# Low part one place later at the norms, and the layer norms' last sums moved from GpSimd to TensorE

## The chip, the cores and the metric

The kernel runs on one core of a Trainium2 chip. The time is device microseconds of one execution, from the first to the last instruction and what lies around them. The engines are TensorE (PE; PEld is its weight load), VectorE (DVE), ScalarE (ACT), GpSimd (POOL) and SyncE (SP, which issues the DMAs of the weight stream).

## What is computed

Two transformer stacks, one behind the other, on 512 tokens of width 1024, in float32. The first has two layers (a mixer of gated linear attention and sparse attention, a gated spatial mixer, and a squared-ReLU MLP after each), with a root-mean-square norm before and after every part. The second has one layer with layer norms: neighbourhood and windowed attention behind a joint input projection, an output projection, and an MLP. What matters for the change are the norms:

```python
def _rms_norm(x, g):
    y = xf * lax.rsqrt(jnp.mean(xf * xf, axis=-1, keepdims=True) + NORM_EPS)
    return (y * g).astype(x.dtype)

h = h + _rms_norm(m, norm_g[layer, 1])                       # first stack
f = _squared_relu_mlp(_rms_norm(h, norm_g[layer, 2]), ...)
h = h + _rms_norm(f, norm_g[layer, 3])

def layer_norm(x, g, b):                                     # second stack
    mu = jnp.mean(xf, axis=-1, keepdims=True)
    xc = xf - mu
    var = jnp.mean(xc * xc, axis=-1, keepdims=True)
    y = xc * lax.rsqrt(var + LN_EPS) * g + b
h = layer_norm(x, ln0_g, ln0_b)
h = layer_norm(ALPHA * h + attn_out, ln1_g, ln1_b)
h = layer_norm(ALPHA * h + ffn_out, ln2_g, ln2_b)
```

## The kernel before

Activations lie transposed: 128 partitions by 8 blocks of the width (KC = 8) by 512 tokens. Weights come as a stream of 321 panels of 128 by 1024 through a ring of four places. Every float32 operand is split in a high and a low part: for a panel ScalarE copies the high part (`act_split`, L321) and VectorE subtracts it for the low part (`dve_split`, L328); a product is then three matmuls (high by high, high by low, low by high). "Split q" below is that of the panel q of the next stage. TensorE signals a panel's end with `panel_done`, VectorE a split with `lo_done`.

The order on every engine is written out by hand, and semaphores join the engines. The stages are mix0 (three of them), ffn0, sgu_in, sgu_out, ffn1, mix2_in, mix2_gate, mix2_branch, mix2_out and ffn2. Between two stages stands a norm, and to keep TensorE at work the tokens are taken in two halves of 256 (`half(s)`): the last four panels of a stage run as a tail (`pe_tail`), first for half 0 and then for half 1, while the norm of half 0 goes on; the first four panels of the next stage run as a quad (`pe_quad`), first half 0 block by block and then half 1. `pe_quad` puts a number of constant products of the identity into an unused bank ahead of each half (`pe_hold`, L442, counts in `HOLD`, L444), before it waits for the first block.

Root-mean-square boundary (`dve_boundary`, `act_boundary`; r = 0, 1, 2 stand before ffn0, sgu_in and ffn1). Once the root of a half is there, VectorE takes the reciprocal (`dve_post_rs`, L545), and for each of eight blocks the scale (`dve_post_scale`, L548), the add into h (`dve_post_add`, L553) and the low part of the block before (`lo`, L562). ScalarE makes the high part in between (`hi`, L589). `STEPS` (L411) is VectorE's order, with the four splits and the tail's sums among them; "last" is the low part of block 7.

Layer norm m = 0 (before mix2_in, on h), 1 (before ffn2, on h), 2 (the end, on acc). The mean: GpSimd adds blocks into `part` (`pool_mean_full`, L668, for the first four blocks at full width where m > 0; `pool_mean_half`, L678, one block of a half), and TensorE multiplies `part` and the last block by a matrix of 1/1024 (`pe_mean`, L683 and L685). VectorE subtracts (`dve_centre`, L691), ScalarE squares (`act_var_square`, L698), GpSimd adds the squares of blocks 0, 2, 4, 6 (`pool_var`, L707), and TensorE sums the odd ones and that sum (`pe_var`, L713 and L715). Then the root on ScalarE (`act_var_sd`, L720), the reciprocal (`dve_var_rs`, L725) and the scale (`dve_norm`, L728) on VectorE, the high part and the bias on ScalarE (`act_ln_out`, L733, L736), and the low part on GpSimd (`pool_ln_lo`, L740).

The ends that matter: at m = 0 the norm behind ffn1 (r = 3: `act_post_square`, `pool_post_half`, `pe_post`, `act_post_sd`, `dve_post_rs`, and VectorE's `post3`, L2380) runs into the layer norm, and halves of both are interleaved by hand in all engines' lists (GpSimd L1211 to L1240, TensorE from L1611, ScalarE from L1937, VectorE from L2391). At m = 1 and 2, `pe_ln` hands the mean and the squares to the tail and the quad as things to do after a given part, and `dve_ln` is VectorE's order.

GpSimd's queue also issues DMAs: behind the adds of boundary r = 1 those of wst and bs, and behind `pool_var` of m = 0 those of the rope table and the first biases of the neighbourhood attention.

## Time and profile before

| | us |
|---|---|
| median of 3 runs | 2292.1 |
| lowest and highest | 2281.51, 2295.62 |
| the profiled execution | 2285.85 |
| its span, first to last instruction | 2283.9 |
| TensorE busy in the span | 2201.7 (96%) |
| VectorE busy | 1103.5 (48%) |
| ScalarE busy | 852.5 (37%) |
| GpSimd busy | 237.3 (10%) |
| mean granted TensorE clock, as a share of full speed | 0.983 |

The profile is of one execution. A time in it counts from the span's start. A matmul's end is modelled, so neighbouring matmuls overlap in it; the distance of two starts is the better measure. A constant or float32 product is recorded as two matmuls. In the timeline the bracket at a line's end holds the idle time of the engine before it and what ended it. Idle time of an engine off the path costs nothing.

### The profile page before, as it was taken

How to read it: one execution, taken by the hardware profiler on the slowest of the kernel's cores; microseconds unless marked ns; L12 is line 12 of the kernel's file. 1: busy time of each engine (PE TensorE's matmuls, PEld its weight loads, DVE VectorE, ACT ScalarE, POOL GpSimd, SP SyncE). 2: the span in 40 equal slices, each digit the busy share in tenths (PEclk: the TensorE clock that was granted, in tenths of full speed). 3: DMA queues.
4: the chain of work that ended last, by engine and by line, in shares of the span. 5: the costliest groups of instructions: out<-in, count | busy, mean ns of one | idle time of the engine just before them, and what ended most of it. 6: DMA issues, size and time to landing. Idle time of an engine off the chain costs nothing.

```text
span 2283.9 us, 28971 instructions
## 1 busy us (share of the span) xinstructions
PE 2201.7 (96%) x11040; PEld 1801.1 (79%) x11040; DVE 1103.5 (48%) x1798; ACT 852.5 (37%) x1411; POOL 237.3 (10%) x220
## 2 busy tenths in 40 slices
PE   7998989999999999999999999999999999999997
PEld 5877768888888788889888888876677788888886
DVE  5546555633433736626443445545544445443344
ACT  6324433432323433324332232533476326232232
POOL 2001002010001100310100003401100123000002
PEclk9999988999999999999999999999999999999999
DMA  4223000333222232222332322221111222322331
GB/s 165 90 68 93 19 10 28 102 93 102 92 92 92 93 102 82 86 92 74 102 101 92 94 90 81 84 73 51 34 49 47 83 84 65 111 93 92 100 93 37
DMA packets 52400, 184.51 MB, mean 81 GB/s; under 512 B 5904, under 2 KB 8096, under 8 KB 52288
## 3 DMA queue, kind: packets, MB, share of 16 engines
q1 hardware_dynamic: 49968, 173.39, 24.0%
q0 software_dynamic: 2320, 9.55, 1.3%
q8 instruction: 79, 1.29, 0.2%
q14 instruction: 33, 0.27, 0.0%
HBM read 180.82 MB, written 2.10 MB: 80 GB/s over the span
## 4 chain that ended last, share of the span: by engine, by line
PE 86%; DVE 8%; ACT 3%; POOL 1%; issue 1%; DMA 0%; SPq 0%; ACTq 0%; DVEq 0%; POOLq 0%
PE ps L354 55%; PE ps L941 4%; PE ps L908 3%; PE ps L929 3%; PE ps L1586 3%; PE ps L431 3%; PE ps L1508 3%; PE ps L463 2%; PE ps L919 2%; DVE ring L328 2%; DVE h L553 1%; DVE xa L562 1%; PE ps L1381 1%; ACT ring L321 1%; PE ps L1481 1%
## 5 line engine op out<-in xcount | busy, mean ns | idle before, releaser
L354 PE MATMUL ps<-xa,ring 128*128 128x512 f32 x3192 | 738.9, 391 | 0.0
L354 PEld LDWEIGHTS ps<-xa,ring 128*128 128x128 f32 x3192 | 598.2, 188 | 127.2 <-issue 3.0
L321 ACT ACTIVATE ring<-raw 128x1024 fp32r<-128x1024 f32 x321 | 337.7, 1054 | 513.3 <-PE ps L354 415.8
L328 DVE TENSOR_TENSOR ring<-raw,ring 128x1024 fp32r<-128x1024 f32 x321 | 409.5, 1277 | 245.7 <-ACT ring L321 245.2
L354 PE MATMUL ps<-xb,ring 128*128 128x512 f32 x2208 | 517.2, 395 | 0.0
L354 PEld LDWEIGHTS ps<-xb,ring 128*128 128x128 f32 x2208 | 414.4, 188 | 100.5
L835 DVE TENSOR_TENSOR ffsq<-relu 128x512 f32<-128x512 f32 x96 | 66.3, 691 | 180.3 <-ACT relu L794 180.2
L852 DVE TENSOR_TENSOR acc<-acc,ps 128x512 f32<-128x512 f32 x68 | 46.8, 688 | 207.7 <-PE ps L354 207.7
L941 PE MATMUL ps<-xa,ring 128*128 128x512 f32 x432 | 118.6, 413 | 0.0
L463 PE MATMUL ps<-xa,ring 128*128 128x256 f32 x768 | 97.1, 285 | 11.6 <-POOL xa L740 5.4
L941 PEld LDWEIGHTS ps<-xa,ring 128*128 128x128 f32 x432 | 77.9, 192 | 37.9 <-issue 23.5
L463 PEld LDWEIGHTS ps<-xa,ring 128*128 128x128 f32 x768 | 93.4, 191 | 15.9 <-POOL xa L740 7.4
L794 ACT ACTIVATE relu<-ps 128x512 f32<-128x512 f32 x64 | 38.1, 595 | 180.8 <-PE ps L354 180.8
L838 DVE TENSOR_TENSOR xb<-ffsq,xb 128x512 fp32r<-128x512 f32 x96 | 66.5, 692 | 76.0 <-ACT xb L786 76.0
L1508 PE MATMUL ps<-ring,xa 128*128 128x512 f32 x384 | 90.8, 397 | 2.6 <-DVE xa L562 2.5
L1508 PEld LDWEIGHTS ps<-ring,xa 128*128 128x128 f32 x384 | 72.4, 191 | 20.0 <-DVE xa L562 4.4
L431 PE MATMUL ps<-xb,ring 128*128 128x256 f32 x576 | 70.2, 283 | 0.0
L431 PEld LDWEIGHTS ps<-xb,ring 128*128 128x128 f32 x576 | 69.3, 188 | 0.5
L1017 DVE RECIPROCAL stat<-stat 128x1 f32<-128x1 f32 x128 | 20.9, 163 | 100.1 <-PE ps L929 98.4
L516 POOL TENSOR_TENSOR part<-part,xf 128x512 f32<-128x512 f32 x8 | 14.3, 1793 | 496.7 <-ACT xf L500 496.7
L786 ACT ACTIVATE xb<-ffsq 128x512 fp32r<-128x512 f32 x96 | 59.9, 624 | 11.9 <-DVE ffsq L835 11.7
L969 ACT ACTIVATE n_p<-ps,stat 128x128 f32<-128x128 f32 (+3 forms) x64 | 33.7, 527 | 77.1 <-DVE stat L1005 76.8
(334 smaller groups left out, 2442.5 us busy)
## 6 DMA issues: line engine op xcount, KB each, us to landing
raw<-in_stream SPq DMA_DIRECT2D x321, 512.0 KB, 3.5
c_w<-in_cmp_w POOLq DMA_DIRECT2D x8, 512.0 KB, 4.2
t<-in_rpb POOLq DMA_DIRECT2D x8, 448.0 KB, 3.6
h<-in_x SPq DMA_DIRECT2D x8, 256.0 KB, 8.4
out_y<-h SPq DMA_DIRECT2D x16, 128.0 KB, 1.9
cons<-in_con SPq DMA_DIRECT2D x1, 738.0 KB, 4.3
wst<-in_w_s POOLq DMA_DIRECT2D x1, 512.0 KB, 4.6
bs<-in_b_s POOLq DMA_DIRECT2D x1, 512.0 KB, 5.3
```

The costliest lines, as they stand in the source:

```text
L321: nc.scalar.activation(ring[:, m % RING, 0], raw[:, m % RING], ACT.Copy).then_inc(hi_done, 1)
L328: nc.vector.tensor_tensor(ring[:, m % RING, 1], raw[:, m % RING], ring[:, m % RING, 0].bitcast(F32), ALU.subtract).then_inc(lo_done, 1)
L354: mm = nc.tensor.matmul(bank[:, :], ring[:, n % RING, w, k * P:(k + 1) * P], operand[:, k, xx], start=(i == 0 and w == 0 and xx == 0), sto ...
L431: mm = nc.tensor.matmul(ps[bank][:, half(q % 2)], ring[:, n % RING, w, k * P:(k + 1) * P], operand[:, k, xx, half(s)], start=(k == 0 and w ...
L463: mm = nc.tensor.matmul(ps[QUAD[c]][:, half(s)], ring[:, (n0 + k // 2) % RING, w, at_w:at_w + P], xa[:, k, xx, half(s)], start=(k == 0 and ...
L835: nc.vector.tensor_tensor(ffsq[:, j % 2], relu[:, j % 2], relu[:, j % 2], ALU.mult)\
L838: nc.vector.tensor_tensor(xb[:, j, 1], ffsq[:, j % 2], xb[:, j, 0].bitcast(F32), ALU.subtract).then_inc(sem("ff_lo"), 1)
L908: mm = nc.tensor.matmul(bank[:, 0:nk], q, k, start=True, stop=not masks)
L929: mm = nc.tensor.matmul(ps[2][:, 0:HD], turned[:, u_ % 2, j * P:(j + 1) * P], v[j], start=(j == 0), stop=(j == nk // P - 1))
L941: mm = nc.tensor.matmul(ps[BANK[n]][:, :], ring[:, n % RING, w, k * P:(k + 1) * P], operand[:, k, xx], start=(k == 0 and w == 0 and xx == ...
L1508: mm = nc.tensor.matmul(ps[V_BANKS[g][t]][:, :], xa[:, k, xx, t * P:(t + 1) * P], ring[:, n % RING, w, (k % 2) * T:(k % 2) * T + T], start ...
L1586: mm = nc.tensor.matmul(ps[BANK[n]][:, :].rearrange("p (t d) -> p t d", t=TB), ring[:, n % RING, w, k * P:(k + 1) * P], y_block(KC * i + k ...
```

## The change

- In `dve_boundary` the add of a block comes right behind its scale, and the low part of the block before comes after both. The order in `STEPS` stays.
- The mean of a layer norm: `pool_mean_half` goes. At m = 0 TensorE multiplies all eight blocks of a half by the mean matrix, each as it is ready; at m = 1 and 2 it takes GpSimd's `part` (blocks 0 to 3) and then blocks 4 to 7.
- The squares: `pool_var` goes; TensorE sums all eight.
- `HOLD`: ffn0 and ffn1 (0, 4) to (0, 3), mix2_in (10, 9) to (7, 9), ffn2 (5, 9) to (3, 3).
- At m = 0, half 0 of the layer norm comes ahead of half 1 of the norm behind ffn1: on TensorE its squares before `pe_post(3, 1)`, on ScalarE its root before that one's, on VectorE centring before split 0, and reciprocal and scales before the post norm's reciprocal and first two blocks.
- At m = 1 and 2, the squares of half 1 are summed after block 5 of the next quad's half 0 instead of after block 7 (at the end there is no quad; they stand behind the mean as before).

```diff
@@ -160,7 +160,7 @@
 MIX_AT = {4: (0,), 5: (1,), 6: (2, 3), 7: (4,), 8: (5, 6), 9: (7,), 10: (8, 9), 11: (10,), 12: (11,), 13: (12,), 14: (13,),
           15: (14, 15)}
 PRE_AT = {"ffn0": KC, "sgu_in": 3 * KC, "ffn1": 5 * KC}
-MEAN_PART = (0, 12, 21)
+MEAN_PART = (0, 0, 3)
 
 
 def blocks_beside(i, count, units):
@@ -441,7 +441,7 @@
             for _ in range(count):
                 nc.tensor.matmul(bank[:, :], ident, cons[:, CON["scan"]:CON["scan"] + HT], start=True, stop=True)
 
-        HOLD = {"ffn0": (0, 4), "ffn1": (0, 4), "mix2_in": (10, 9), "ffn2": (5, 9)}
+        HOLD = {"ffn0": (0, 3), "ffn1": (0, 3), "mix2_in": (7, 9), "ffn2": (3, 3)}
 
         def pe_quad(pe, name, ready, after):
 
@@ -572,9 +572,9 @@
                         dve_post_rs(dve, chain, r, s)
                     elif what == "step":
                         dve_post_scale(dve, r, s, i, g_post)
+                        dve_post_add(dve, r, s, i)
                         if i >= 1:
                             lo(s, i - 1)
-                        dve_post_add(dve, r, s, i)
                     elif what == "last":
                         lo(s, KC - 1)
                     elif what == "out":
@@ -668,22 +668,15 @@
                 nc.gpsimd.tensor_tensor(part[:, :], src[:, 0] if k == 1 else part[:, :], src[:, k], ALU.add)\
                     .then_inc(sem("mean_part"), 1)
 
-        def pool_mean_half(pool, m, s, k, src, ready):
-
-            pool.wait_ge(*ready)
-            first = m == 0 and k == 1
-            if not first:
-                done = (6 * s + k - 1) if m == 0 else (3 + 3 * s + k - 4)
-                pool.wait_ge(sem("mean_part"), MEAN_PART[m] + done)
-            nc.gpsimd.tensor_tensor(part[:, half(s)], src[:, 0, half(s)] if first else part[:, half(s)],
-                                    src[:, k, half(s)], ALU.add).then_inc(sem("mean_part"), 1)
-
         def pe_mean(pe, m, s, src, ready):
-            pe.wait_ge(sem("mean_part"), MEAN_PART[m] + (6 * s + 6 if m == 0 else 3 * s + 6))
-            nc.tensor.matmul(ps[2 - 2 * s][:, half(s)], mean_w, part[:, half(s)], start=True, stop=False)
-            pe.wait_ge(*ready)
-            nc.tensor.matmul(ps[2 - 2 * s][:, half(s)], mean_w, src[:, KC - 1, half(s)], start=False, stop=True)\
-                .then_inc(sem("mean_summed"), 1)
+            if m > 0:
+                pe.wait_ge(sem("mean_part"), MEAN_PART[m] + 3)
+                nc.tensor.matmul(ps[2 - 2 * s][:, half(s)], mean_w, part[:, half(s)], start=True, stop=False)
+            for k in range(0 if m == 0 else 4, KC):
+                pe.wait_ge(*ready(k))
+                mm = nc.tensor.matmul(ps[2 - 2 * s][:, half(s)], mean_w, src[:, k, half(s)], start=(m == 0 and k == 0),
+                                      stop=k == KC - 1)
+            mm.then_inc(sem("mean_summed"), 1)
 
         def dve_centre(dve, m, s, k, src):
             if k == 0:
@@ -697,23 +690,11 @@
                 act.wait_ge(sem("var_summed"), 2 * m + 1)
             nc.scalar.activation(squares[:, k], h[:, k, half(s)], ACT.Square).then_inc(sem("var_sq"), 1)
 
-        def pool_var(pool, m, s, squares):
-
-            for k in range(2, KC, 2):
-                pool.wait_ge(sem("var_sq"), 16 * m + 8 * s + k + 1)
-                done = 6 * m + 3 * s + k // 2 - 1
-                if k > 2:
-                    pool.wait_ge(sem("var_part"), done)
-                nc.gpsimd.tensor_tensor(part[:, half(s)], squares[:, 0] if k == 2 else part[:, half(s)], squares[:, k],
-                                        ALU.add).then_inc(sem("var_part"), 1)
-
         def pe_var(pe, m, s, squares):
-            for k in range(1, KC, 2):
+            for k in range(KC):
                 pe.wait_ge(sem("var_sq"), 16 * m + 8 * s + k + 1)
-                nc.tensor.matmul(ps[6 + s][:, half(s)], mean_w, squares[:, k], start=k == 1, stop=False)
-            pe.wait_ge(sem("var_part"), 6 * m + 3 * s + 3)
-            nc.tensor.matmul(ps[6 + s][:, half(s)], mean_w, part[:, half(s)], start=False, stop=True)\
-                .then_inc(sem("var_summed"), 1)
+                mm = nc.tensor.matmul(ps[6 + s][:, half(s)], mean_w, squares[:, k], start=k == 0, stop=k == KC - 1)
+            mm.then_inc(sem("var_summed"), 1)
 
         def act_var_sd(act, m, s):
             act.wait_ge(sem("var_summed"), 2 * m + s + 1)
@@ -1211,17 +1192,8 @@
             for q in range(3):
                 pool_post_half(pool, 3, 0, q)
 
-            def mean0(s, k):
-                pool_mean_half(pool, 0, s, k, h, (sem("h_ready"), 48 + 8 * s + k + 1))
-
-            for k in range(1, 5):
-                mean0(0, k)
-            pool_post_half(pool, 3, 1, 0)
-            pool_post_half(pool, 3, 1, 1)
-            mean0(0, 5)
-            mean0(0, 6)
-            pool_post_half(pool, 3, 1, 2)
-            pool_var(pool, 0, 0, lnsq)
+            for q in range(3):
+                pool_post_half(pool, 3, 1, q)
             pool.wait_ge(panel_done, BASE["ffn1"] + 64)
             pool.dma_start(ropes[:, :, :], rope).then_inc(sem("rope_in"), 16)
 
@@ -1232,9 +1204,6 @@
             load_rpb(1)
             for k in range(KC):
                 pool_ln_lo(pool, 0, 0, k)
-            for k in range(1, 7):
-                mean0(1, k)
-            pool_var(pool, 0, 1, lnsq)
             for k in range(KC):
                 pool_ln_lo(pool, 0, 1, k)
             for hd in range(8):
@@ -1255,19 +1224,10 @@
             def pool_ln(m, name, src, lo):
                 n0 = tail_base(name)[0]
                 pool_mean_full(pool, m, src, lambda k: (taken["dve"], READS["dve"][n0 - 4 + k + 1]))
-                for k in range(4, 7):
-                    pool_mean_half(pool, m, 0, k, src, (sem("tail_out"), tail_base(name)[1] + (k - 4) // 2 + 1))
-                for k in range(4, 6):
-                    pool_mean_half(pool, m, 1, k, src, (taken["dve"], READS["dve"][n0 + 2]))
-                pool_var(pool, m, 0, xfh)
-                pool_mean_half(pool, m, 1, 6, src, (taken["dve"], READS["dve"][n0 + 4]))
                 if lo:
-                    for k in range(KC):
-                        pool_ln_lo(pool, m, 0, k)
-                pool_var(pool, m, 1, xfh)
-                if lo:
-                    for k in range(KC):
-                        pool_ln_lo(pool, m, 1, k)
+                    for s in range(2):
+                        for k in range(KC):
+                            pool_ln_lo(pool, m, s, k)
 
             pool_ln(1, "mix2_out", h, True)
             pool_ln(2, "ffn2", acc, False)
@@ -1608,13 +1568,13 @@
                         mm.then_inc(sem("tail_a"), 1)
             pe_ffn(pe, "ffn1", pre_ready("ffn1"), sums(2)[1], 2, sums(3)[0])
 
-            pe_mean(pe, 0, 0, h, (sem("h_ready"), 48 + KC))
+            pe_mean(pe, 0, 0, h, lambda k: (sem("h_ready"), 48 + k + 1))
+            pe_var(pe, 0, 0, lnsq)
             pe_post(pe, 3, 1)
-            pe_var(pe, 0, 0, lnsq)
 
             def quad0(s, k):
                 if s == 0 and k == 7:
-                    pe_mean(pe, 0, 1, h, (sem("h_ready"), 48 + 2 * KC))
+                    pe_mean(pe, 0, 1, h, lambda i: (sem("h_ready"), 48 + KC + i + 1))
                     pe_var(pe, 0, 1, lnsq)
 
             pe_quad(pe, "mix2_in", ln_ready(0), quad0)
@@ -1674,14 +1634,14 @@
 
                 def tail(s, q):
                     if s == 1 and q == 0:
-                        pe_mean(pe, m, 0, src, (sem("tail_out"), t0 + 2))
+                        pe_mean(pe, m, 0, src, lambda k: (sem("tail_out"), t0 + k // 2 - 1))
                     if s == 1 and q == 2:
                         pe_var(pe, m, 0, xfh)
 
                 def quad(s, k):
                     if s == 0 and k == 1:
-                        pe_mean(pe, m, 1, src, (taken["dve"], READS["dve"][n0 + 4]))
-                    if s == 0 and k == 7:
+                        pe_mean(pe, m, 1, src, lambda i: (taken["dve"], READS["dve"][n0 + 2 * (i // 2) - 2]))
+                    if s == 0 and k == 5:
                         pe_var(pe, m, 1, xfh)
 
                 return tail, quad
@@ -1689,7 +1649,7 @@
             tail, quad = pe_ln(1, "mix2_out", h)
             pe_tail(pe, "mix2_out", xs, tail)
             pe_ffn(pe, "ffn2", ln_ready(1), quad, None, pe_ln(2, "ffn2", acc)[0])
-            pe_mean(pe, 2, 1, acc, (taken["dve"], READS["dve"][BASE["ffn2"] + 64]))
+            pe_mean(pe, 2, 1, acc, lambda k: (taken["dve"], READS["dve"][BASE["ffn2"] + 60 + 2 * (k // 2) - 2]))
             pe_var(pe, 2, 1, xfh)
 
         @block.scalar
@@ -1936,8 +1896,8 @@
             split_to("mix2_in", 0)
             for k in range(KC):
                 act_var_square(act, 0, 0, k, lnsq)
+            act_var_sd(act, 0, 0)
             act_post_sd(act, 3, 1)
-            act_var_sd(act, 0, 0)
             for k in range(KC):
                 act_ln_out(act, 0, 0, k, "ln0_b")
                 if k in (0, 2, 5):
@@ -2391,15 +2351,15 @@
                 post3(0, k)
                 if k in (3, 7):
                     dve_tail(dve, "ffn1", 1, k // 4, acc)
-            split_to("mix2_in", 0)
             for k in range(KC):
                 dve_centre(dve, 0, 0, k, h)
+            split_to("mix2_in", 0)
+            dve_var_rs(dve, chain, 0, 0)
+            for k in range(KC):
+                dve_norm(dve, 0, 0, k, "ln0_g")
             dve_post_rs(dve, chain, 3, 1)
             post3(1, 0)
             post3(1, 1)
-            dve_var_rs(dve, chain, 0, 0)
-            for k in range(KC):
-                dve_norm(dve, 0, 0, k, "ln0_g")
             for k in range(2, KC):
                 post3(1, k)
                 if k in (2, 4, 6):
```

## Rows read from the trace of the kernel before

**Rows 1.** The page: the chain of work that ended last, by engine.
```profile
PE 86%; DVE 8%; ACT 3%; POOL 1%; issue 1%; DMA 0%; SPq 0%; ACTq 0%; DVEq 0%; POOLq 0%
```

**Rows 2.** Timeline at ffn0's norm, second half of the tokens: start us, us, engine.
```profile
405.02 0.48 DVE L548 SCALAR_TENSOR_TENSOR acc<-acc,vecs,ps 128x256 f32<-128x256 f32 x1
...
405.54 0.42 DVE L553 TENSOR_TENSOR h<-h,acc 128x256 f32<-128x256 f32 x1
...
405.88 0.47 DVE L548 SCALAR_TENSOR_TENSOR acc<-acc,vecs,ps 128x256 f32<-128x256 f32 x1
...
406.54 0.48 DVE L562 SCALAR_TENSOR_TENSOR xa<-h,vecs,xa 128x256 fp32r<-128x256 f32 x1 [0.18 <-ACT xa L589]
...
407.93 0.49 DVE L562 SCALAR_TENSOR_TENSOR xa<-h,vecs,xa 128x256 fp32r<-128x256 f32 x1 [0.18 <-ACT xa L589]
...
415.87 1.22 DVE L328 TENSOR_TENSOR ring<-raw,ring 128x1024 fp32r<-128x1024 f32 x1 [1.52 <-ACT ring L321]
...
417.41 0.48 DVE L562 SCALAR_TENSOR_TENSOR xa<-h,vecs,xa 128x256 fp32r<-128x256 f32 x1
...
417.94 3.13 PE L463 MATMUL ps<-xa,ring 128*128 128x256 f32 x24 [1.96 <-DVE xa L562]
```

**Rows 3.** Timeline at sgu_in's norm.
```profile
780.95 10.08 PE L1508 MATMUL ps<-ring,xa 128*128 128x512 f32 x36 [2.22 <-DVE xa L562]
...
791.93 1.12 PE L1539 MATMUL ps<-part,cons 128*128 128x512 f32 x2 [0.91 <-DVE part L2281]
```

**Rows 4.** Windows: busy us and counts of PE, PEld, DVE, ACT, POOL, granted clock, DMA.
```profile
405.00:421.00 16.00, 13.85 (x107) 13.09 (x106) 12.26 (x27) 7.26 (x12) 0.00 (x0) 1.00 0.12 34
...
783.00:784.00 1.00, 1.00 (x4) 0.81 (x3) 1.00 (x2) 1.00 (x2) 0.00 (x0) 0.50 0.63 152
...
1415.00:1421.00 6.00, 6.00 (x15) 4.66 (x16) 4.41 (x10) 3.65 (x10) 2.62 (x4) 0.53 0.31 87
```

**Rows 5.** Timeline: constant products ahead of mix2_in (two records each).
```profile
1421.74 4.48 PE L442 MATMUL ps<-cons 128*128 128x256 f32 x20
```

**Rows 6.** Timeline at ffn1's end and mix2_in.
```profile
1414.94 1.22 PE L683 MATMUL ps<-part,cons 128*128 128x256 f32 x2 [3.47 <-POOL part L678]
...
1417.06 2.74 DVE L691 TENSOR_TENSOR h<-h,ps 128x256 f32<-128x256 f32 x8 [0.15 <-PE ps L685]
...
1421.94 0.45 ACT L720 ACTIVATE ps<-ps,cons 128x256 f32<-128x256 f32 x1 [1.43 <-PE ps L715]
...
1427.69 1.68 PE L463 MATMUL ps<-xa,ring 128*128 128x256 f32 x12 [1.47 <-POOL xa L740]
...
1429.13 1.22 DVE L328 TENSOR_TENSOR ring<-raw,ring 128x1024 fp32r<-128x1024 f32 x1
...
1432.03 1.76 DVE L328 TENSOR_TENSOR ring<-raw,ring 128x1024 fp32r<-128x1024 f32 x1
...
1443.40 0.70 PE L683 MATMUL ps<-part,cons 128*128 128x256 f32 x2 [2.07 <-POOL part L678]
...
1450.49 0.45 ACT L720 ACTIVATE ps<-ps,cons 128x256 f32<-128x256 f32 x1 [2.74 <-PE ps L715]
...
1455.20 11.77 PE L463 MATMUL ps<-xa,ring 128*128 128x256 f32 x96 [0.33 <-POOL xa L740]
```

**Rows 7.** Timeline at mix2_out's end and ffn2.
```profile
1892.89 0.45 ACT L720 ACTIVATE ps<-ps,cons 128x256 f32<-128x256 f32 x1 [3.27 <-PE ps L715]
...
1914.05 0.45 ACT L720 ACTIVATE ps<-ps,cons 128x256 f32<-128x256 f32 x1 [5.40 <-PE ps L715]
...
1918.76 11.77 PE L463 MATMUL ps<-xa,ring 128*128 128x256 f32 x96 [0.86 <-POOL xa L740]
```

**Rows 8.** Timeline at the end of ffn2, the last norm.
```profile
2267.19 0.68 DVE L493 TENSOR_TENSOR acc<-acc,ps 128x512 f32<-128x512 f32 x1
...
2269.90 2.73 DVE L691 TENSOR_TENSOR h<-acc,ps 128x256 f32<-128x256 f32 x8 [0.46 <-PE ps L685]
...
2275.00 0.45 ACT L720 ACTIVATE ps<-ps,cons 128x256 f32<-128x256 f32 x1 [1.92 <-PE ps L715]
```

## The prediction

> **What bounds the kernel now.** I read the chain of work that ended last first: 86% of it is TensorE, 8% VectorE [rows 1]. So a norm costs only what TensorE waits in it, and the change touches six norms: at ffn0, sgu_in and ffn1 (root mean square), at mix2_in, ffn2 and the end (layer norms). Then the timelines at the norms, and the windows for the granted clock.
>
> At ffn0, in the second half of the tokens, VectorE runs scale, low part, add for each block. A block takes 1.39 us (406.54 to 407.93), of which part is a wait for ScalarE's high part [rows 2]. TensorE keeps up until block 6, stands idle 1.96 us, and starts at 417.94 when that block's low part is done [rows 2]. At sgu_in the same gap is 2.22 us, and a second one stands at 791.93, behind sums on VectorE [rows 3]. ffn1 repeats ffn0 with the same 1.96 us.
>
> At mix2_in TensorE is idle 3.47 us before the first mean product (so its tail ended at 1411.47) and 2.07 us before the second half's [rows 6]. Here the clock matters: behind the first gap the window from 1415 to 1421 has a granted clock of 0.53, and the one from 783 at sgu_in 0.50, the lower level of 1.2 GHz; round ffn0's gap of 1.96 us it stays 1.00 [rows 4].
>
> **Prices.** A constant product is two records; 20 records take 4.48 us, the last one's own 0.38 included, so one product takes 0.43 us at the full clock [rows 5]. A block of twelve matmuls takes 1.48 us (96 in 11.77 [rows 6]).
>
> **Edit 1, low part one place later.** Now the add stands right behind its scale, which it needs: 0.52 us from start to start (405.02 to 405.54), then 0.34 to the next (405.88) [rows 2]. The low part is as long as the scale, 0.48, and overlaps alike: 0.40. The wait for ScalarE goes, since a high part of a whole period earlier is asked for. The new period is 0.52 + 0.34 + 0.40 = 1.26. Add 1 ends at 405.88 + 0.52 + 0.42 = 406.82 and add 6 five periods later at 413.1, where it ended at 414.36 (405.96 and six periods): 1.26 us earlier. The split behind it (415.87) moves with it, since ScalarE's copy follows high part 6 at once. Of step 7, low part 6 stood 0.40 behind the scale and now stands 0.52 + 0.34 = 0.86 behind: 0.46 later. Net **−0.8 us** at ffn0 and again at ffn1. The next stop is low part 7, some 0.6 us behind low part 6 and hidden by TensorE's block 6 (1.48). In the first half each of seven steps pays 0.13 us for the add behind its scale, less the waits for ScalarE that go (about 0.8): nothing on VectorE; TensorE's last two blocks there start up to 0.6 us later, which the one constant product fewer (0.43) gives back ahead of the second half. Without that cover it is +0.2. If waits and stalls cancel in the second half too, the gain is nothing; if low part 6 were not delayed it is −1.3.
>
> At sgu_in the wait that ends last is another: high part 7, two splits, copies and squares on ScalarE and sums on VectorE lead to 791.93 [rows 3]. They start with add 7, which gains 1.26 and another 0.27 (0.79 to 0.52 behind its scale). TensorE's own work ahead of 791.93 comes in 0.9 + 0.8 us earlier, so it can use it: **−1.5 us** (between −0.8 and −1.7). The loads of wst and bs on GpSimd's queue wait for the same adds and move with them; nothing else is queued there.
>
> **Edit 2, TensorE sums.** 42 sums leave GpSimd (18 at mix2_in, 12 at each other layer norm) and 42 products come to TensorE: per half 8 + 8 for 2 + 5 at mix2_in, 5 + 8 for 2 + 5 elsewhere. 13 constant products go: 41 of these four stages become 28.
>
> mix2_in, first half: the eight mean products can start at 1411.47, since all but the last block of h is added by then: 8 × 0.43 = 3.45, centring at 1414.95 for 1417.06. TensorE now waits for h block by block, with the squares, the other half's sum and mix2_in queued behind it; VectorE adds the last block some 0.3 us after 1411.47, seven products early, so nothing waits. The gap of 3.47 us goes, and with it the low clock. First square 0.9 behind, eight products, 0.2 of drain: the root at 1419.5 for 1421.94 [rows 6]. From root to TensorE's first block it is 4.71 us where nothing stands between (1914.05 to 1918.76 [rows 7]), here 5.75 since the other half's reciprocal and two steps stood there; they now stand behind. So block 0 starts at 1424.2 for 1427.69, 3.5 us earlier. But this doesn't last. Block 2 needs the split of the next panel, and VectorE reaches it only behind its reciprocal and the eight norm products (1419.5 + 0.5 + 1.8 + 8 × 0.39 = 1424.9), the other half's reciprocal (1.8), three scales and two adds (1.9): at 1428.6, done between 1429.8 and 1430.4. That is where it was before (1429.13 + 1.22 = 1430.35 [rows 6]). From there VectorE's pace, some 3.3 us for each of two further splits (1430.35 to 1433.8), rules as before, and TensorE ends two blocks behind the last split: 1430.1 + 2 × 3.35 + 3.0 = 1439.8, for 1441.33 (1443.40 less 2.07 [rows 6]). GpSimd's mean is not waited for: centring at 1439.8 + 3.6 = 1443.4, root 4.55 later at 1448.0 for 1450.49, block 0 at 1452.7 for 1455.20. **−2.5 us**. The new gap ahead of block 2, some 2.6 us, is longer than that of sgu_in, so I expect the low level behind it; it slows blocks that wait for the splits anyway, so it costs 0.1 to 1: **−2.4**. If nothing held, the gain would be 3.8 us; if the splits slip by a microsecond and the clock falls in both halves, it is nothing.
>
> Here the Trainium skill speaks against the change. A split takes 1.22 us with GpSimd at rest [rows 2] and once beside its low parts, but 1.76 there at 1432.03 [rows 6]. The GPSIMD Engine Reference (section 1, Specifications) says that GpSimd shares its SBUF interfaces with VectorE and contends with VectorE instructions that have two SBUF inputs. By that rule all splits moved beside low parts take 1.76 and the term is −1.9; by the 1.22 alone it is −2.9. The trace agrees with the rule in one of the two splits.
>
> The rope and bias loads on GpSimd's queue come some 7 us earlier, once its sums ahead of them are gone. They meet no panel load that is waited for: four panels have landed. Price nothing.
>
> ffn2: TensorE's tail carries three products more at the mean (+1.3), so centring starts 1.3 later; eight products behind one another end 0.2 sooner than four, a wait for GpSimd and a fifth, and the root goes from 1892.89 to 1894.0 [rows 7]. GpSimd has no sum left in front of its first low part, so block 0 starts 4.71 later, at 1898.7, where the profile has 1898.96. Two blocks (2.96) and five mean products (2.15) lead to 1903.8. The squares are now summed behind block 5, not 7: 1903.8 + 4 × 1.48 = 1909.7, then 3.45 + 0.2, root at 1913.35 for 1914.05: **−0.7 us** (+0.6 if the squares, due at 1909.75, come late; −1 at best). The holds ahead of it fall from 9 to 3, and TensorE waits some 0.7 us in place of 0.86 [rows 7].
>
> The end: the mean +1.3 and the squares +0.6 (three products less a wait for GpSimd and its sum) shift the first half's root by 1.9; the tail's sum on VectorE moves from 2267.19 to 2269.1 [rows 8]. Three mean products run ahead of it and GpSimd's sum is gone, but VectorE's tail sum (0.6) and other four norm products (1.6) now stand ahead of the centring: 2271.3 for 2269.90. From centring to root it was 5.1 us, at the low clock, and is 4.55 at the full one: 2275.85 for 2275.00. **+0.9 us** (0 to +2.6, the latter if the clock falls: eight products at half speed for some 3.4 us, as long as it lasted at sgu_in, cost 1.7).
>
> **Sum.** −0.8 − 1.5 − 0.8 − 2.4 − 0.7 + 0.9 = −5.3 us. Against the profiled execution's own 2285.85 us: 2280.5. The runs shown have a median of 2292.1 and a lowest of 2281.51; with the profiled one the middle of four is 2289.0. A new set of runs may fall anywhere there, so I put the level at 2289 and forecast 2284.
>
> **Rivals.**
> 1. *Slower: TensorE becomes the bound at the layer norms.* 42 products more and 13 fewer are 29 × 0.43 = 12.5 us. For it: each stands in TensorE's order, blocks behind it wait. Against it: in every layer norm TensorE has gaps of 0.9 to 3.5 us [rows 6, 7]. It decides where the products exceed the gap they fill, as in the tails of ffn2. All on the path: 2289 + 12.5 = 2301. Chance 0.08.
> 2. *The reordering does nothing*: the add's stall eats the wait that goes. Then −5.3 + 3.1 = −2.2: 2287. For it: 0.13 us stall against a 0.18 us wait. Against: the period is a sum of starts seen. Chance 0.17.
> 3. *The clock falls in the waits*, which have fewer constant products: five stretches at 1.7 us each, −5.3 + 8.5 = +3.2: 2292. For it: the gaps of 2.2 and 3.5 us. Against: ffn0's 1.96, and most new gaps are about 1 us. Chance 0.15.
> 4. *The full gain at mix2_in* (3.8, splits not in the way): 2282. Against: the walk above. Chance 0.05.
>
> The forecast has 0.55; its own range is 2276 to 2291, mostly the spread of the runs shown (14 us). The range goes from there up to rival 3: 2275 to 2295; rival 1 is left out. About 1% (23 us) is what a measurement can tell from no change. Only rival 1 with high runs or a low set could pass it: faster 0.02, same 0.95, slower 0.03.
>
> **What would show it.** Right: at ffn0 low parts 1.26 us apart and a gap near 1.2 us where 1.96 was; at mix2_in centring at once behind eight products, a wait for VectorE's split ahead of block 2, clock 1.00 in the second half's squares; at the end the last root about 0.9 later relative to the last panel. Wrong: low parts still 1.4 apart; block 2 following block 1 without a wait; a granted clock near 0.5 behind gaps of 1 us; a total off by over 8 us, which no walk here would explain.

## The result, and the profile after

| | before | after |
|---|---|---|
| median of 13 runs | 2286.91 us (2280.94 to 2296.55) | 2276.5 us (2271.09 to 2280.44) |
| profiled execution | 2285.85 us | 2271.93 us |
| its span; mean granted clock | 2283.9 us; 0.983 | 2270.2 us; 0.992 |

The ratio after to before is 0.9946, 95% interval [0.9928, 0.9964]. That is inside the 1% that was called no change, and 2276.5 us is inside the forecast's range, but the gain is 10.4 us by the medians where 5.3 were worked out. The changed kernel was measured twice more, each time with new runs of before beside it: 0.9962 [0.9949, 0.9975] and 0.9967 [0.9956, 0.9978], that is 8.7 and 7.5 us of 2283. The median of before was 2286.91 us here and 2282.51 to 2283.78 us in the four later sets of 29 to 33 runs, so some 3 to 4 of the 10.4 us look like this set's own and not the change's.

The two profiled spans differ by 13.7 us. This table cuts both at the same matmuls of TensorE's order; each entry is a difference of two starts in the trace, and behind it the time in that stretch at the lower of the clock's two levels.

| TensorE from ... to ... | before, us (low) | after, us (low) | difference |
|---|---|---|---|
| start to the output product ahead of ffn0 (code untouched) | 360.85 (29.0) | 356.51 (18.8) | -4.3 |
| ffn0's norm, to its first quad's end | 59.93 (8.5) | 59.43 (8.5) | -0.5 |
| sgu_in's norm | 63.34 (3.4) | 61.59 (0) | -1.75 |
| ffn1's norm | 52.55 (0) | 51.30 (0) | -1.25 |
| mix2_in's norm and quad | 79.02 (13.7) | 77.59 (3.4) | -1.45 |
| neighbourhood attention (untouched) | 137.62 (6.8) | 134.42 (0) | -3.2 |
| windowed attention, gates, to mix2_out (untouched) | 219.02 (6.8) | 217.45 (3.4) | -1.6 |
| ffn2's norm and quad | 61.95 (0) | 61.19 (0) | -0.75 |
| ffn2's last panels and the end | 44.34 (9.9) | 45.41 (3.9) | +1.1 |

All other stretches agree within 0.03 us. The touched ones give -4.6 us where the forecast had -5.3, each with the sign it was given. The rest, -9.1 us in this pair, stands in three stages whose code is the same.

**The profile after.** The granted clock and the chain that ended last, by engine: TensorE's share is 88%, where it was 86 [rows 1].

```profile
core 0: 2270.2 us, clock 0.992
PE 88%; DVE 8%; ACT 3%; issue 1%; POOL 0%; DMA 0%; SPq 0%; ACTq 0%; DVEq 0%
```

ffn0's norm after, second half of the tokens (timeline: start us, us, engine, line, operation; L548 is the scale, L553 the add, L562 the low part, L463 the quad's blocks):

```profile
403.63 0.42 DVE L553 TENSOR_TENSOR h<-h,acc 128x256 f32<-128x256 f32 x1
403.97 0.48 DVE L562 SCALAR_TENSOR_TENSOR xa<-h,vecs,xa 128x256 fp32r<-128x256 f32 x1
404.37 0.47 DVE L548 SCALAR_TENSOR_TENSOR acc<-acc,vecs,ps 128x256 f32<-128x256 f32 x1
404.88 0.42 DVE L553 TENSOR_TENSOR h<-h,acc 128x256 f32<-128x256 f32 x1
405.22 0.48 DVE L562 SCALAR_TENSOR_TENSOR xa<-h,vecs,xa 128x256 fp32r<-128x256 f32 x1
...
412.56 0.48 DVE L562 SCALAR_TENSOR_TENSOR xa<-h,vecs,xa 128x256 fp32r<-128x256 f32 x1
413.09 3.13 PE L463 MATMUL ps<-xa,ring 128*128 128x256 f32 x24 [0.95 <-DVE xa L562]
```

The period is 1.25 us (403.97 to 405.22), where the forecast had 1.26 and before had 1.39 [rows 2]. No wait for ScalarE is left in it. TensorE's gap is 0.95 us for 1.96.

mix2_in after. L677 are the mean products, L684 the centring, L696 the squares' products, L701 the root, L442 constant products, L328 VectorE's part of a weight split:

```profile
1403.46 3.62 PE L677 MATMUL ps<-h,cons 128*128 128x256 f32 x16
1407.12 2.74 DVE L684 TENSOR_TENSOR h<-h,ps 128x256 f32<-128x256 f32 x8 [2.24 <-PE ps L677]
1411.80 0.45 ACT L701 ACTIVATE ps<-ps,cons 128x256 f32<-128x256 f32 x1 [1.50 <-PE ps L696]
1416.51 1.69 PE L463 MATMUL ps<-xa,ring 128*128 128x256 f32 x12 [0.86 <-POOL xa L721]
1421.37 1.21 DVE L328 TENSOR_TENSOR ring<-raw,ring 128x1024 fp32r<-128x1024 f32 x1
1422.64 10.38 PE L463 MATMUL ps<-xa,ring 128*128 128x256 f32 x72 [2.54 <-DVE ring L328]
1424.26 1.75 DVE L328 TENSOR_TENSOR ring<-raw,ring 128x1024 fp32r<-128x1024 f32 x1
1427.54 1.21 DVE L328 TENSOR_TENSOR ring<-raw,ring 128x1024 fp32r<-128x1024 f32 x1
1432.86 3.62 PE L677 MATMUL ps<-h,cons 128*128 128x256 f32 x16
1436.52 2.74 DVE L684 TENSOR_TENSOR h<-h,ps 128x256 f32<-128x256 f32 x8 [6.70 <-PE ps L677]
1441.20 0.45 ACT L701 ACTIVATE ps<-ps,cons 128x256 f32<-128x256 f32 x1 [1.50 <-PE ps L696]
1445.91 7.34 PE L463 MATMUL ps<-xa,ring 128*128 128x256 f32 x59 [0.86 <-POOL xa L721]
```

The whole kernel reaches mix2_in 7.85 us sooner after, so 7.85 is to be added to compare with [rows 6]. The gap of 3.47 us is gone. In its place TensorE waits 2.54 us for VectorE's split ahead of block 2, as forecast, and behind that wait the clock is low; windows (busy us of PE, PEld, DVE, ACT, POOL, then granted clock, DMA share, GB/s):

```profile
1422.50:1427.00 4.50, 4.36 (x24) 4.36 (x25) 4.50 (x9) 2.50 (x5) 3.75 (x4) 0.62 0.38 117
1441.00:1446.00 5.00, 4.14 (x20) 3.33 (x18) 4.29 (x8) 2.39 (x6) 0.73 (x1) 1.00 0.01 3
```

The end after (L493 adds the tail's last sums; L684 and L701 as above):

```profile
2244.26 0.69 DVE L493 TENSOR_TENSOR acc<-acc,ps 128x512 f32<-128x512 f32 x1 [0.84 <-PE ps L431]
2250.49 0.45 ACT L701 ACTIVATE ps<-ps,cons 128x256 f32<-128x256 f32 x1 [4.43 <-PE ps L696]
2254.35 0.68 DVE L493 TENSOR_TENSOR acc<-acc,ps 128x512 f32<-128x512 f32 x1
2256.51 2.73 DVE L684 TENSOR_TENSOR h<-acc,ps 128x256 f32<-128x256 f32 x8
2261.28 0.45 ACT L701 ACTIVATE ps<-ps,cons 128x256 f32<-128x256 f32 x1 [1.58 <-PE ps L696]
```

From the tail's sum to the last root it is 6.93 us (2254.35 to 2261.28), where it was 7.81 (2267.19 to 2275.00 [rows 8]); the first half's root comes 0.6 later behind its own sum, and the mean products 1.3 later: +1.3 + 0.6 - 0.9 = +1.0. That is against this profile of before. The last stretch took 353.55 us there and in one other profile of before's order, counted from ffn2's first panel behind its quad, and 354.4 to 354.5 us in the seven others, with 12 to 15 us low for 9.9; after has 354.62 us. Against those seven the end lost 0.1 to 0.3 us.

### The profile page after: what moved, and what is told of

Same layout as the page of the kernel before. It is cut to its first block, busy times and chain, and to the rows that moved or that the text cites. A ratio compares the mean times of both kernels' runs of the same rounds, so it can differ in the third digit from the quotient of the medians.

```text
span 2270.2 us, 29011 instructions
## 1 busy us (share of the span) xinstructions
PE 2196.7 (97%) x11098; PEld 1800.7 (79%) x11098; DVE 1102.7 (49%) x1798; ACT 853.3 (38%) x1411; POOL 202.8 (9%) x178
## 4 chain that ended last, share of the span: by engine, by line
PE 88%; DVE 8%; ACT 3%; issue 1%; POOL 0%; DMA 0%; SPq 0%; ACTq 0%; DVEq 0%
PE ps L354 56%; PE ps L922 4%; PE ps L889 3%; PE ps L431 3%; PE ps L910 3%; PE ps L1546 3%; PE ps L1468 3%; PE ps L463 2%; PE ps L900 2%; DVE ring L328 1%; PE ps L696 1%; DVE acc L548 1%; DVE h L553 1%; PE ps L1341 1%; ACT ring L321 1%
## 5 line engine op out<-in xcount | busy, mean ns | idle before, releaser
L328 DVE TENSOR_TENSOR ring<-raw,ring 128x1024 fp32r<-128x1024 f32 x321 | 408.0, 1273 | 242.5 <-ACT ring L321 242.1
L463 PE MATMUL ps<-xa,ring 128*128 128x256 f32 x768 | 98.9, 288 | 10.9 <-DVE ring L328 3.5
L463 PEld LDWEIGHTS ps<-xa,ring 128*128 128x128 f32 x768 | 95.0, 194 | 15.3 <-POOL xa L721 4.9
L767 ACT ACTIVATE xb<-ffsq 128x512 fp32r<-128x512 f32 x96 | 59.8, 623 | 10.7 <-DVE ffsq L816 10.4
L1546 PE MATMUL ps<-yhi,ring 128*128 128x512 f32 x192 | 60.5, 395 | 0.0
```

The source lines that it names most:

```text
L328: nc.vector.tensor_tensor(ring[:, m % RING, 1], raw[:, m % RING], ring[:, m % RING, 0].bitcast(F32), ALU.subtract).then_inc(lo_done, 1)
L463: mm = nc.tensor.matmul(ps[QUAD[c]][:, half(s)], ring[:, (n0 + k // 2) % RING, w, at_w:at_w + P], xa[:, k, xx, half(s)], start=(k == 0 and ...
L1546: mm = nc.tensor.matmul(ps[BANK[n]][:, :].rearrange("p (t d) -> p t d", t=TB), ring[:, n % RING, w, k * P:(k + 1) * P], y_block(KC * i + k ...
```

## The experiments

**Theory 1**, after the result: the edits do what the walk said, and the rest is the clock in attention stages. Rivals: the edits are worth more than reckoned; the two sets of runs differ by luck; the holds matter. The first four ran side by side (before there: median 2283.56 us of 33 runs).

**The kernel before, unchanged**, as a measure of what two equal kernels differ by.

> The kernel before, unchanged, for more executions and a second profile. Theory A (the gain beyond the 4.6 us found in the changed norms is clock time in the attention stages that has nothing to do with the change): single executions lie anywhere from 2281 to 2297 us, and between two of them the time differs by about half of the difference in time at the low clock; ratio 1.000 +-0.002. Theory B (the low clock in the attention stages of before is fixed by the kernel): the second profile shows the low level at the same places as the first, 2285 to 2290 us in the median.

2282.07 us, ratio 0.9992 [0.9977, 1.0007]. Its stages repeat those of before within 0.05 us, attention with its low stretches too (137.57 and 219.02 us), but for the first: 356.84 us (18.8 low) where before had 360.85 (29.0). So the first row of the table above, -4.3 us, comes and goes between executions of one kernel and is no gain of the change. The attention rows repeat in these two profiles of before; of after's three profiles, further down, one does not repeat the others. The low stretches stood at the same places, as theory B of this run had it, but its median of 2285 to 2290 was not reached.

**The low part one place later, alone.**

```diff
                         dve_post_scale(dve, r, s, i, g_post)
+                        dve_post_add(dve, r, s, i)
                         if i >= 1:
                             lo(s, i - 1)
-                        dve_post_add(dve, r, s, i)
```

> Only the low part one place later in the three boundaries; everything else as before. Theory A, by the places read from the two profiles: ffn0 -0.5, sgu_in -1.8, ffn1 -1.2, together -3.5 us, ratio 0.9985. Theory B (the gaps made shorter also keep the clock up in most executions): -6 us or more, ratio 0.997 or less, and a mean granted clock above that of before.

2279.57 us, ratio 0.9979 [0.9969, 0.9989], between the two theories. (The profile is of its slowest execution, 2285.19 us.) ffn1's norm took 51.30 us, the change's whole 1.25. At sgu_in the sums reach TensorE 24.12 us behind the reciprocal (764.37 to 788.49), in before 25.70 (766.23 to 791.93): 1.6 sooner. But that norm's stretch gained only 0.3 (63.02 us), for now the low clock stood behind the wait instead of before it:

```profile
778.24 8.46 PE L1508 MATMUL ps<-ring,xa 128*128 128x512 f32 x36 [1.37 <-DVE xa L562]
788.49 1.12 PE L1539 MATMUL ps<-part,cons 128*128 128x512 f32 x2 [1.79 <-DVE part L2281]
790.48 9.80 PE L1508 MATMUL ps<-ring,xa 128*128 128x512 f32 x36
```

36 matmuls took 8.46 us ahead of the wait and 9.80 behind it; in before 10.08 ahead of it [rows 3]. And the neighbourhood attention took 139.91 us, 2.3 more than in before. So what an edit saves ahead may be lost behind.

**All but that: the layer norms, alone** (the low part's place and the holds of ffn0 and ffn1 as before).

> All of the change but the low part's place (and the constant products of ffn0 and ffn1, which stay at 4). Theory A: mix2_in -1.4, ffn2 -0.7, end +1.1, together -1.0 us, ratio 0.9995. Theory B (the low clock behind mix2_in's long gaps was the larger part, in more places than one profile shows): -5 us or more, ratio 0.998 or less.

2278.71 us, ratio 0.9976 [0.9965, 0.9986]. mix2_in 77.58 us (-1.45), ffn2 61.18, the end +1.0, as in after. At sgu_in, where and ahead of which this kernel is still as before, the stretch took 65.45 us, 2.1 more than before, with 4.5 us low; attention 135.09. By the medians both halves of the change gain, about 5 us each, and together 8 to 10. But the three layer norms give only some 1.1 of the 5.5 us: the ratio is the one of theory B, and in the profile (2282.3 us, among the slower executions) the other gain is 4.1 us in the two attention stages, whose code is before's.

sgu_in shows the same in a smaller way. From its norm to sgu_out's last panels, with before's code there and ahead of it, five profiles took 292.2 us with 3.4 us low, and four, this one among them, 295.4 to 295.5 us with 6.8 us low.

**The changed kernel with the old holds** (10, 9 at mix2_in, 5, 9 at ffn2, 4 for 3 at ffn0 and ffn1).

```diff
-        HOLD = {"ffn0": (0, 3), "ffn1": (0, 3), "mix2_in": (7, 9), "ffn2": (3, 3)}
+        HOLD = {"ffn0": (0, 4), "ffn1": (0, 4), "mix2_in": (10, 9), "ffn2": (5, 9)}
```

> The changed kernel with the constant products of before (4, 4, 10 and 9, 5 and 9). Theory A (the constant products end before the operand comes): as the changed kernel where they fit, later where they don't: ffn2's nine products of 3.9 us stand in a wait of some 2 us, so +2 us there and +0.5 at mix2_in, ratio to before 0.9955 to 0.996. Theory B (fewer constant products let the clock fall): faster than the changed kernel, ratio below 0.9945.

2277.73 us, ratio 0.9972 [0.9962, 0.9982]. ffn2 took 62.97 us for 61.19: nine constant products are longer than the wait they fill now. No other stage is longer by its counts. sgu_in, whose own code is that of after, took 1.6 us more with 3.4 us low behind its wait, and the ratio is above the 0.9955 to 0.996 that was expected.

**The changed kernel again**, with three others (before there: 2282.97 us of 29 runs).

> The changed kernel as it is, for a comparison beside the parts on one chip and a second profile. Theory A (each half of the change keeps its own gain, and the constant products taken out add the rest): the low part alone gave 0.9979 and the sums alone 0.9976, so 0.9945 to 0.9955. Theory B (the first comparison was a lucky one): 0.997 to 0.998, the 4.6 us of the changed norms alone. The profile: the six norms' stages as in the first profile to 0.1 us, except sgu_in; the neighbourhood attention anywhere from 134.4 to 140 us, by where the low clock falls.

2274.53 us, ratio 0.9962 [0.9949, 0.9975]; attention 134.33 and 217.42 us, every touched stage within 0.2 of the first profile.

**The changed kernel with before's order at mix2_in** (the other half's post norm ahead of the layer norm's squares, root, reciprocal and scales, split 0 ahead of the centring).

> The changed kernel with the order of before at mix2_in: on TensorE the other half's sum ahead of the squares, on VectorE its reciprocal and first two blocks ahead of the layer norm's reciprocal. Theory A (the split of the next panel is what ends the wait, so the move changes nothing behind block 1): mix2_in's stage within 0.5 us of the changed kernel's 77.6, ratio as the changed kernel. Theory B (the move carries mix2_in's gain): 1.4 us or more longer there, as long as before (79.0).

2280.86 us, ratio 0.9992 [0.9983, 1.0001]: 6.3 us more than its neighbour. At mix2_in itself it lost 1.05 us (78.62), between the 0.5 and the 1.4 of the two theories. The neighbourhood attention, in which nothing was changed, took 143.59 us, 9.3 more.

**Where that time is.** In all these kernels TensorE has one gap of 2.29 us in the neighbourhood attention, some 55 us into it (the others there are 0.8 us or less, but for one of 1.2 us at its end): the transposes of a score unit wait for its probabilities. After has it too:

```profile
1557.09 0.66 PE L900 MATMUL ps<-cons,a_p 128*128 128x128 f32 x4 [2.29 <-ACT a_p L950]
```

The windows of the 7 us behind it, in before, after, and after with the old order, one line each:

```profile
1566.38:1573.38 7.00, 7.00 (x26) 4.92 (x26) 2.60 (x6) 3.12 (x7) 0.00 (x0) 0.58 0.00 0
```
```profile
1557.09:1564.09 7.00, 7.00 (x36) 4.90 (x37) 4.10 (x10) 3.02 (x7) 0.00 (x0) 1.00 0.00 0
```
```profile
1559.04:1566.04 7.00, 7.00 (x28) 4.97 (x28) 2.59 (x6) 3.14 (x7) 0.00 (x0) 0.61 0.00 0
```

The same gap, the same work behind it, and a granted clock of 0.58, 1.00 and 0.61 (the level of 1.2 GHz for most of the window in two of them): 36 matmuls done in one, 26 and 28 in the others. **Theory 2**: whether the clock falls behind a given gap hangs on when the kernel arrives there, and a microsecond or two of work ahead of it decide. Rival: the change itself makes the attention faster by some other way (buffers, weight splits that come sooner).

**mix2_in's gaps filled in the kernel before**: eight and five constant products ahead of its two mean products.

```diff
+            pe_free(pe, BASE["mix2_in"] + 1)
+            pe_hold(pe, ps[3][:, half(0)], 8)
             pe_mean(pe, 0, 0, h, (sem("h_ready"), 48 + KC))
...
+                    pe_hold(pe, ps[3][:, half(1)], 5)
                     pe_mean(pe, 0, 1, h, (sem("h_ready"), 48 + 2 * KC))
```

> The kernel before with eight constant products in mix2_in's gap of 3.47 us and five in that of 2.07 us, so that the clock stays up; sums on GpSimd as before. Theory A (of mix2_in's gain the kept clock is the larger part): clock 1.00 from 1414 to 1452, the stage 1.5 us shorter than before's 79.0, ratio 0.999 or less. Theory B (the gain is that TensorE doesn't wait for GpSimd): within 0.4 us of 79.0.

2282.38 us, ratio 0.9997 [0.9988, 1.0006]. mix2_in took 77.75 us with no low clock at all, 1.3 less than before and only 0.15 more than the change, with GpSimd's sums still there; attention 134.41 and 217.44 as in after, with before's code. So the attention's time is reached without any of the change's edits. In this profile 3.2 us were given back at sgu_in (65.51, 4.6 low, 1.1 more behind it) and 0.8 at the end. That stretch of sgu_in lies ahead of the edit, so the loss there is one more case of an untouched norm going the slow way. The total did not reach the 0.999 or less that was expected.

**Five constant products in the attention of before**, meant for the 2.29 us gap.

```diff
         def pe_turn(pe, u_, probs):
             nk = UNITS[u_][5]
+            if u_ == U_NA + NA_END[0] + 2:
+                pe.wait_ge(sem("at_turned"), u_ - 1)
+                pe_hold(pe, ps[6 + u_ % 2][:, half(0)], 5)
```

> The kernel before with five constant products in the gap of 2.29 us in the neighbourhood attention (behind the first rotation on VectorE), which the change doesn't touch. Theory A (the low clock behind this gap costs 3.2 us in some executions and none in others, by when it falls): the stage at 134.4 us, no low clock in it, median 1.5 to 3 us below before, ratio 0.9987 to 0.9993, and a narrower spread. Theory B (it is no part of the difference): ratio 1.000 and the stage at 137.6 us.

2285.47 us, ratio 1.0018 [1.0007, 1.0028]. I had named the wrong unit: the products began 21 us ahead of the gap, which stayed.

```profile
1549.46 2.32 PE L442 MATMUL ps<-cons 128*128 128x256 f32 x10
...
1573.14 0.66 PE L922 MATMUL ps<-cons,a_p 128*128 128x128 f32 x4 [2.29 <-ACT a_p L972]
```

So it says nothing of the gap's filling; it is a delay of 2.15 us. Less those, the stage took 135.1 us for 137.6, with no low clock behind the gap.

**Delays alone** (before there: 2282.51 us of 31 runs). Between mix2_in's quad and the attention TensorE has no wait; a few constant products there change nothing but the time of arrival.

```diff
+            pe_free(pe, M2 + 4)
+            pe_hold(pe, ps[0][:, half(0)], 4)
             for i in range(4, 12):
                 n = M2 + i
                 pe_panel(pe, n, xa)
```

Four in the kernel before:

> The kernel before with four constant products (1.7 us of TensorE) more at the start of the panels behind mix2_in's first four, a stretch in which TensorE has no wait. Theory (arrival): what the neighbourhood attention takes hangs on when the kernel arrives there; 1.7 us later puts the kernel before where the changed one arrives in relation to its low stretches, so that stage takes 134.4 to 135.1 us in place of 137.6 and the next 217.4 in place of 219.0: the total is 1 to 3 us shorter although TensorE has 1.7 us more to do. Rival (the change's own edits made the attention faster): attention stays at 137.6 and the total is 1.7 us longer.

Three in the changed kernel:

> The changed kernel with three constant products (1.3 us) more at the same place. Theory (arrival): it now arrives about where the run with the old order at mix2_in did, so the neighbourhood attention takes 137 to 144 us in place of 134.4, and the total is 4 to 10 us longer for 1.3 us of work. Rival (own edits): attention stays at 134.4, total 1.3 us longer.

Two in the kernel before:

> The kernel before with two constant products (0.9 us) more at the same place. Theory (arrival): attention differs from 137.6 us by something other than nothing, since the arrival is one that no kernel here has had; its size is open (134.4 to 143.6 are what other arrivals gave). Rival (own edits): attention stays at 137.6, total 0.9 us longer.

And the products of the experiment above in the changed kernel, at the same wrong unit:

> The changed kernel with five constant products (2.2 us) in TensorE's gap of 2.3 us in the neighbourhood attention, ahead of the score unit that waits for the first rotation. Theory (arrival and that gap): the changed kernel already passes the gap with no low clock in that stage, so the filling costs nothing there but brings nothing: attention 134.3 to 134.6 us, total 0 to 1 us longer. Rival (the gap still costs something in the changed kernel): attention 133.5 or less and total 1 us shorter.

| kernel | added, us | median, us | neighbourhood attention (low), us | next stage |
|---|---|---|---|---|
| before, its profile | 0 | 2286.91 | 137.62 (6.8) | 219.02 |
| before + 2 | 0.9 | 2285.68 | 141.26 (18.5) | 218.28 |
| before + 4 | 1.7 | 2282.81 | 136.28 (4.0) | 218.74 |
| after, its profile | 0 | 2276.5 | 134.42 (0) | 217.45 |
| after + 3 | 1.3 | 2280.1 | 137.61 (6.9) | 218.99 |
| after + 5 at the wrong unit | 2.2, in the stage | 2279.94 | 140.13 (7.9), 138.0 without them | 218.49 |

Three products of 0.43 us put the changed kernel's attention where before's was, to 0.01 us. The rows of the weight panels' matmuls that TensorE takes beside the attention units, with shortest, median and longest in ns and their first and last start (after, after with three, before with two):

```profile
L922 PE MATMUL ps<-xa,ring x432: 387/393/504, 1502.4 to 1756.8; 128*128 128x512 f32 x144
```
```profile
L922 PE MATMUL ps<-xa,ring x432: 387/393/794, 1503.4 to 1762.5; 128*128 128x512 f32 x144
```
```profile
L941 PE MATMUL ps<-xa,ring x432: 387/394/794, 1506.8 to 1770.4; 128*128 128x512 f32 x144
```

254.4, 259.1 and 263.6 us for the same 432 matmuls; before's is 259.1. The longest one took 504 ns in the first and 794, twice the median of 393 or 394, in the others. The rival falls from both sides: with all of the change's edits in it the attention can be as slow as before's, and with none of them (mix2_in's gaps filled) as fast as after's.

How far this shows that the delay decides is another matter. Each row of the table is one profile. The four kernels with delays ran on one chip, on which neither before nor after was profiled, and after itself took 2 us more in one of three profiles (further down). The medians speak for the delay only weakly: before with two 1.0009 [0.9993, 1.0024], after with three 0.9986 [0.9965, 1.0007] where after alone was 0.9962 and 0.9967 elsewhere, and the intervals overlap. The clearest pair is after and after with the old order, side by side on one chip: 134.33 and 143.59 us in the attention, and 0.9962 [0.9949, 0.9975] and 0.9992 [0.9983, 1.0001] in the total. So it is shown that the same attention code takes either time, and supported, not proven, that the arrival decides which.

Of the sizes two were missed: before with four was to reach 134.4 to 135.1 us and reached 136.3, so its total was not below before's: it carries 1.7 us more of work in the same time (2282.81 and 2282.51); and after with the misplaced five, which was to lose at most a microsecond, lost 3 to 5 by the medians, which theory 2 allows once they are seen as a delay, but did not forecast.

**The gap itself filled**, by the same five products five units further on, beside the changed kernel (before there: 2283.78 us of 29 runs).

```diff
-            if u_ == U_NA + NA_END[0] + 2:
+            if u_ == U_NA + NA_END[0] + 7:
```

The changed kernel, unchanged; then it, before, and before with two products more, each with the gap filled:

> The changed kernel, unchanged, as a measure for its neighbours. Theory (arrival): neighbourhood attention 134.4 us if it arrives as in its two profiles so far; total 2271 to 2277 us. Rival (its gain was luck of two sets): 2279 or more.

> The changed kernel with five constant products (2.2 us) right in TensorE's 2.3 us gap ahead of the seventh score unit behind the first rotation. Theory (the gap costs only where low clock follows it): attention 134.3 to 134.5 us, total as the changed kernel or up to 2 us shorter at the median, since executions that fell low there no longer do. Rival (the gap is not what lets the clock fall): total as the changed kernel's, and low clock may still stand behind it.

> The kernel before with the same gap filled. Theory (gap and arrival): no low clock some 55 us behind the attention's start, the stage takes 134.3 to 134.6 us in place of 137.6, and the total is 3 us shorter or more. Rival (the low clock comes from the arrival alone or from another gap): the stage stays at 137 or more.

> The run that was slowest in the attention of those with a delay (before with two constant products more behind mix2_in: 141.3 us), now with the gap filled. Theory (gap and arrival): 134.3 to 134.6 us, total 5 us or more below its own run without the filling (2285.7, and before's median moves with the chip). Rival: 137 or more.

| kernel | median, us | ratio to before | neighbourhood attention (low), us |
|---|---|---|---|
| after | 2275.24 | 0.9967 [0.9956, 0.9978] | 136.42 (4.4) |
| after, gap filled | 2274.55 | 0.9957 [0.9940, 0.9973] | 134.42 (0) |
| before, gap filled | 2280.08 | 0.9985 [0.9969, 1.0001] | 134.42 (0) |
| before + 2, gap filled | 2282.0 | 0.9996 [0.9979, 1.0012] | 135.09 (3.4) |

The slowest case, before with two, without and with the filling: the wait and the window of 7 us behind it.

```profile
1561.47 1.12 PE L919 MATMUL ps<-cons,a_p 128*128 128x128 f32 x4 [2.29 <-ACT a_p L969]
1561.47:1568.47 7.00, 7.00 (x22) 4.98 (x23) 2.60 (x6) 2.52 (x6) 0.00 (x0) 0.50 0.00 0
```
```profile
1559.88 2.32 PE L442 MATMUL ps<-cons 128*128 128x256 f32 x10
1562.34:1569.34 7.00, 7.00 (x36) 4.92 (x37) 4.11 (x10) 3.03 (x7) 0.00 (x0) 1.00 0.00 0
```

The clock stays at 1.00, and 141.26 us become 135.09, 137.62 become 134.42. (The 3.4 us that stay low lie 74 us behind the filled gap.) So the attention's part of the loss is this gap's, when the clock falls behind it. This holds for the stage. The totals are less clear: before with the gap filled is 3.7 us below its neighbours by the medians, with an interval that takes in 1. Before with two and the gap filled missed both of its sizes: 135.09 for 134.3 to 134.6 us, and 3.7 us below its own run without the filling, in another set, where 5 or more were expected. The changed kernel itself, on this chip, was not spared: 136.42 us with a clock of 0.76 in that window, where its first two profiles had 1.00. With the gap filled its stage was back at 134.42; the two medians, 2274.55 and 2275.24, can't be told apart.

## Why the prediction was right or wrong

**The level.** The forecast took 2289 us for before; its new median was 2286.91. That is 2.1 of the 7.5 us that separate 2284 from 2276.5. The other 5.4 are the size of the gain, and of these 3 to 4 are this set's high median of before: beside the later sets the gain is 7.5 to 8.7 us for 5.3.

**ffn0 and ffn1, -0.8 each.** The mechanism was right, and in the second half the size: from the reciprocal (L545) to the last quad blocks 14.71 us before and 13.87 after at ffn1. The first half, costed at nothing, was not: -0.4 at ffn1, +0.3 at ffn0. In both the last two blocks now wait 0.5 us for a low part, so that wait doesn't tell them apart, and what does is not shown. In sum -1.75 for -1.6.

**sgu_in, -1.5.** The walk behind add 7 measured -1.6 in two kernels. What it left out is that the clock's low stretch may stand ahead of that wait, where it is hidden, or behind it, where it costs: -1.75 in after, which had none at all, -0.3 with the low part's edit alone.

**mix2_in, -2.4, measured -1.45.** The first half went as walked: centring at 1407.12 + 7.85 = 1414.97 (forecast 1414.95), root 1419.65 (1419.5), block 0 1424.36 (1424.2), block 2 behind the split at 1430.49 (1429.8 to 1430.4). The step that failed is the next: two further splits were to rule to the half's end "as before", with the low clock hidden behind them at 0.1 to 1 us. They didn't rule in before either. There TensorE ran the last seven blocks without a wait, in 1.48 us each, and was done 4.1 us behind the last split (1435.47 + 1.76), where the forecast took 3.0 (and 3.35 us a split, where 1430.35 to 1433.8 is 3.45):

```profile
1430.99 10.33 PE L463 MATMUL ps<-xa,ring 128*128 128x256 f32 x84 [1.62 <-POOL xa L740]
```

In after the splits ended at 1426.01 and 1428.75, within half a microsecond of the forecast's times, and again TensorE waited for neither. Its 72 matmuls took 10.38 us for 8.9 at the full clock, 1.5 more, above the bound. The second half's mean products started at 1432.86 + 7.85 = 1440.7; less those 1.5 us it would be 1439.2 (an estimate), 0.6 ahead of the forecast's 1439.8. So 0.6 of the 1.5 us was made up and 0.9 was not. Everything behind is 1.0 to 1.1 us late against the forecast (centring 1444.37 for 1443.4, root 1449.05 for 1448.0, block 0 1453.76 for 1452.7). The clock in the second half's squares stayed 1.00 as forecast. That TensorE no longer waits for GpSimd's mean is not what the gain is shown to be, either: constant products in before's gaps, with GpSimd's sums kept, gave 1.3 of the 1.45 us.

Of the splits' 1.22 or 1.76 us the two beside GpSimd's low parts took 1.21 and 1.75, and the third, behind the last low part, 1.21. The Trainium skill's rule in the GPSIMD Engine Reference (section 1, Specifications), that GpSimd contends with VectorE instructions that have two SBUF inputs, was borne out by one of the two. In before it was borne out by two of three: the split at 1435.47, which the forecast left out, took 1.76 too.

**ffn2, -0.7, measured -0.75.** From root to root 19.25 us (1880.02 to 1899.27) for 19.35 forecast. **The end, +0.9, measured +1.1.** By the same three terms; but it is +0.1 to +0.3 against seven of nine profiles of before's order, which had 2 to 5 us more of low clock there.

**Rival 1** (TensorE becomes the bound, +12.5) fell: 42 products more stood in gaps but for the tails of ffn2. **Rival 2** (the reordering does nothing) fell: the period is 1.25. **Rival 4** fell, with the splits in the way. **Rival 3** was the one that asked the right question, and got the sign and the place wrong. It priced the clock in the waits that the change touches. The total of low time went down instead, from 78 to 38 us, and half of that in stages that I had left at nothing because their code is the same. That is the step that failed for the total: the sum held only the touched stages, which gave -4.6 of the -5.3, and left at nothing the two attention stages, which gave -4.8 in two profiles of after and -1.7 in the third. It needed a term for each gap near 2 us further on, 0 to 9 us wide for the attention's alone (134.3 to 143.6 us in eighteen profiles), of either sign. The trace of before showed it: 6.8 us low behind that gap. With it the forecast of 5.3 would have had a range of its own towards 10.

**What stays open.** Of the 10.4 us by the medians, 4.6 are the touched stages in one pair of profiles; 1.7 to 4.8 are the two attention stages in three profiles of after. What is left, 1 to 4 us, is no more than the high median of before brings in the first set, and is not located in a stage. The first 360 us differ between executions (355 to 362 us with either code), sgu_in with before's code by 3.2 us and the end by 0.9, and profiles of single executions can't tell how often each falls which way. Whether the change shifts that mix is not shown. Nor is it shown what makes a given arrival fall low; the changed kernel took 134.42, 134.33 and 136.42 us in three profiles. In the windowed attention, 3.4 us of low clock begin in before 0.8 us behind a gap of 1.18 us (at 1648.62), and after has the gap and no low clock behind it; that this is its 1.6 us is read, and no run filled that gap.

## What to carry to other kernels

Where TensorE is busy 97% of the time, a gap of 2 us costs its own length and, here, another 0 to 9 us in low clock behind it; how much is not fixed by the code of that stage, and one profile doesn't settle it. So a small change is judged stage by stage, by busy gaps and by low time apart, and a gain or loss in an untouched stage is no gain of the edit until unchanged code has been shown not to reach it; filling a gap somewhere else, or a delay of a few constant products, tests that. Filling the gap by constant products just short of it brought the stage to 134.42 us in two kernels and to 135.09 in a third, from 136.4 to 141.3; check in the trace that they stand in the gap, and shrink the fill when the gap shrinks.
